# The fourth layer's Fourier mixer on scaled columns, with the token factor applied behind the feature stage, and a new order in the opening

## The reference

```python
def rms_norm(x, g, eps=RMS_EPS):
    x32 = x.astype(jnp.float32)
    y = x32 * lax.rsqrt(jnp.mean(x32 * x32, axis=-1, keepdims=True) + eps)
    return y.astype(x.dtype) * g

def modulate(x, g, shift, scale):
    return rms_norm(x, g) * (1 + scale) + shift

def fourier_mixer(h, w, bias):
    b, s, d = h.shape
    hg = h.astype(jnp.float32).reshape(b, s, FOURIER_GROUPS, d // FOURIER_GROUPS)
    f = jnp.fft.fft2(hg, axes=(1, 3), norm="ortho").real
    return f.reshape(b, s, d).astype(h.dtype) @ w + bias
...
        sh_a, sc_a, g_a, sh_m, sc_m, g_m = jnp.split(silu_c @ mod_w[i] + mod_b[i], 6, axis=-1)
        h_lat = modulate(x_lat, norm_mix_g[i], sh_a, sc_a)
...
        x_lat = x_lat + g_a * y_lat
        x_lat = x_lat + g_m * sq_relu_mlp(modulate(x_lat, norm_mlp_g[i], sh_m, sc_m), mlp_w1[i], mlp_w2[i])
```

## Time and profile before

| | us |
|---|---|
| executions | 2173.69, 2174.12, 2174.76 |
| median | 2174.12 |
| the profiled execution, its device time | 2173.29 |
| its span in the profile | 2171.4 |
| busy in the span: TensorE, VectorE, ScalarE, GpSimd | 2066.7, 1508.5, 1016.9, 9.2 |
| mean granted clock of TensorE | 0.972 |

### The profile page before, as it was taken

The page is one execution under the profiler, slowest core; times in us unless marked ns, Lnnn a source line. Parts: engine busy times, 40 slices in busy tenths (PEclk is TensorE's granted clock), DMA queues, the critical chain, the costliest instruction groups (busy, mean ns, idle before and its releaser), DMA issues.

```text
span 2171.4 us, 34465 instructions
## 1 busy us (share of the span) xinstructions
PE 2066.7 (95%) x13290; PEld 1832.1 (84%) x13290; DVE 1508.5 (69%) x2301; ACT 1016.9 (47%) x1691; POOL 9.2 (0%) x33
## 2 busy tenths in 40 slices
PE   6999999998999999999988889998999998999998
PEld 4698888887877788888866779998999987899998
DVE  3668668587667586857677868887866774555555
ACT  4362323237666562322336765555644653444443
POOL 0000000000000000000000000000000000000000
PEclk9999999999999999999998999999999997899999
DMA  8847445441112245558551128663465541355553
GB/s 312 304 172 226 145 157 166 153 131 60 59 59 78 86 152 189 176 178 274 186 152 62 35 62 307 233 234 123 156 195 175 164 148 39 117 175 174 174 175 106
DMA packets 254147, 340.37 MB, mean 157 GB/s; under 512 B 23895, under 2 KB 232626, under 8 KB 250946
## 3 DMA queue, kind: packets, MB, share of 16 engines
q1 hardware_dynamic: 254018, 338.60, 46.9%
HBM read 337.52 MB, written 1.05 MB: 156 GB/s over the span
## 4 chain that ended last, share of the span: by engine, by line
PE 79%; DVE 9%; ACT 7%; issue 4%; DMA 0%; SPq 0%; DVEq 0%; POOL 0%; ACTq 0%
PE bank L1624 24%; PE bank L1625 23%; PE bank L1626 23%; PE bank L2399 4%; DVE w_lo L2461 1%; ACT p_raw L1256 1%; PE bank L1676 1%; ACT w_hi L917 1%; DVE norm L2488 1%; ACT p_raw L1244 1%; DVE p_all L2945 1%; PE bank L1695 1%; ACT norm L1010 1%; ACT mp_raw L1422 1%; DVE neg_max L2954 0%
## 5 line engine op out<-in xcount | busy, mean ns | idle before, releaser
L917 ACT ACTIVATE w_hi<-w_raw 128x1024 fp32r<-128x1024 f32 x443 | 462.7, 1052 | 459.6 <-PE bank L1626 459.2
L2461 DVE TENSOR_TENSOR w_lo<-w_raw,w_hi 128x1024 fp32r<-128x1024 f32 x443 | 537.0, 1220 | 42.2 <-ACT w_hi L917 39.3
L1624 PE MATMUL bank<-g_hi,w_hi 128*128 128x256 f32 (+1 forms) x1728 | 549.5, 318 | 7.5 <-DVE g_lo L2999 3.6
L1625 PE MATMUL bank<-g_lo,w_hi 128*128 128x256 f32 (+1 forms) x1728 | 545.3, 316 | 0.0
L1626 PE MATMUL bank<-g_hi,w_lo 128*128 128x256 f32 (+1 forms) x1728 | 545.0, 315 | 0.0
L1624 PE MATMUL bank<-h_hi,w_hi 128*128 128x512 f32 (+3 forms) x1360 | 465.7, 342 | 13.7 <-DVE h_lo L2498 9.9
L1625 PE MATMUL bank<-h_lo,w_hi 128*128 128x512 f32 (+3 forms) x1360 | 459.1, 338 | 0.0
L1626 PE MATMUL bank<-h_hi,w_lo 128*128 128x512 f32 (+3 forms) x1360 | 458.9, 337 | 0.0
L1624 PEld LDWEIGHTS bank<-g_hi,w_hi 128*128 128x128 f32 x1728 | 330.8, 191 | 37.5 <-issue 6.0
L1626 PEld LDWEIGHTS bank<-g_hi,w_lo 128*128 128x128 f32 x1728 | 330.8, 191 | 20.5
L1625 PEld LDWEIGHTS bank<-g_lo,w_hi 128*128 128x128 f32 x1728 | 331.0, 192 | 19.4
(11 more groups left out here) (457 smaller groups left out, 2746.6 us busy)
## 6 DMA issues: line engine op xcount, KB each, us to landing
w_raw<-in_mlp_w SPq DMA_DIRECT2D x128, 1024.0 KB, 5.8
mod_raw<-in_mod_w SPq DMA_DIRECT2D x96, 768.0 KB, 4.7
first_raw<-in_mod_w SPq DMA_DIRECT2D x24, 1024.0 KB, 5.7
w_raw<-in_w_expert_gate SPq DMA_DIRECT2D x16, 1024.0 KB, 5.3
w_raw<-in_w_expert_up SPq DMA_DIRECT2D x16, 1024.0 KB, 5.6
w_raw<-in_w_expert_down SPq DMA_DIRECT2D x16, 1024.0 KB, 5.5
w_raw<-in_diff_w_qkv SPq DMA_DIRECT2D x12, 1024.0 KB, 5.1
w_raw<-in_fourier_w SPq DMA_DIRECT2D x8, 1024.0 KB, 5.7
```

Source lines behind the costliest of these rows:

```text
L917: act.activation(W_hi[n % RING][:, :].rearrange("p (k c) -> p k c", c=P), w_raw[slot][:, :, place, :], ACT.Copy).then_inc(s("w_hi"), 1)
L1624: pe.matmul(dst, w_hi, r_hi, start=start, stop=False)
L1625: pe.matmul(dst, w_hi, r_lo, start=False, stop=False)
L2461: dve.tensor_tensor(W_lo[n % RING][:, :].rearrange("p (k c) -> p k c", c=P), w_raw[slot][:, :, place, :], W_hi[n % RING][:, :].bitcast(F32 ...
```

## The change

In the fourth layer's mixer "mix3" joins the tuple LATE: each column of X is multiplied by its scale, without shift and without the token's factor, as soon as the third MLP has completed it. The feature tiles are made of these columns. token_sum sums the squares into two columns of one number per token, one root and one reciprocal of 128 x 2 follow (token_rstd), and the evacuation of the feature tiles (both parts) multiplies by it, since tokens lie in the partitions there. The shift is transformed by itself: waves_of_shift, six small products inside the last block of the third MLP, gives 8 columns of one number per feature, which are added to token 0 of each difference and sum.

In the opening the fold matrix is loaded ahead of the context; the norm of the rows is made for x first and for the context then; the row products start behind the second unit of the first group; the small vectors are turned behind the last unit of the group; the high and low part of the DFT matrix are made earlier; the scaled columns leave out the edge columns and are waited for one by one; GpSimd makes the low part of the eight output columns; of the three panels split ahead, two are split behind the last column; turning the second group follows the first output panel. SP issues the DFT matrix before the last three units of the first group, and the mixer's two weight units behind six units of the second group instead of ahead of it. ROW_NORMS goes from 6 to 8, the meta tokens' wait for meta_sum from 1 to 2, and the plan's tile counts follow.

```diff
--- before.py
+++ after.py
...
-LATE = ("mlp2", "mlp3", "win", "ffn_2")
+LATE = ("mlp2", "mix3", "mlp3", "win", "ffn_2")
...
-ROWS_AFTER = {2: range(0, 4), 3: range(4, 8), 4: range(8, 12), 5: range(12, 16)}
+ROWS_AFTER = {1: range(0, 3), 2: range(3, 6), 3: range(6, 9), 4: range(9, 12), 5: range(12, 14), 6: range(14, 16)}
 SCALED_AHEAD = [("scale", 0), ("scale", 1), ("sum", 0), ("scale", 2), ("sum", 1), ("scale", 3), ("sum", 2), ("sum", 3)]
-THIRD_GROUP_AT = {0: [0], 1: [1, 2], 2: [3, 4], 3: [5], 4: [6], 5: [7]}
+THIRD_GROUP_AT = {1: [0, 1], 2: [2, 3], 3: [4], 4: [5], 5: [6], 6: [7]}
...
+        shift_waves = sb("shift_waves", [P, 2, GROUPS])
+        token_rstd = sb("token_rstd", [P, 2])
...
+        U_hi = {"mlp2": H_hi, "mix3": H_hi, "mlp3": U3_hi, "win": H_hi[:, :, META:TOK2], "ffn_2": G_hi}
+        U_lo = {"mlp2": H_lo, "mix3": H_lo, "mlp3": U3_lo, "win": H_lo[:, :, META:TOK2], "ffn_2": G_lo}
...
+        def inner(v, m, st):
+
+            return v[:, m, st * LAT:(st + 1) * LAT].rearrange("p (e c) -> p e c", e=2)[:, :, 1:]
...
+            if name == "mix3":
+                return scale_mix[:, k, 0:1]
...
-            sp.dma_start(x_rows[:, 2:4, :], a["ctx"][0].rearrange("(t p) d -> p t d", p=P)).then_inc(s("x_in"), 16)
+            sp.dma_start(first_fold[:, :, :], a["first_fold"].rearrange("p (k c) -> p k c", k=2)).then_inc(s("ctx_in"), 16)
+            sp.dma_start(x_rows[:, 2:4, :], a["ctx"][0].rearrange("(t p) d -> p t d", p=P)).then_inc(s("ctx_in"), 16)
             load_first(range(FIRST_RING))
-            sp.dma_start(first_fold[:, :, :], a["first_fold"].rearrange("p (k c) -> p k c", k=2)).then_inc(s("fold_in"), 16)
...
-            load_first(range(FIRST_RING, MOD_UNITS))
+            load_first(range(FIRST_RING, MOD_UNITS - 3))
             dft_in = a["dft"].rearrange("(k p) (a c) -> p k a c", p=P, a=2)
             for k in range(2):
                 sp.dma_start(dft[:, 2 * k:2 * k + 2, :], dft_in[:, k]).then_inc(s("dft_in"), 16)
+            load_first(range(MOD_UNITS - 3, MOD_UNITS))
...
+            load_first(range(MOD_UNITS, 2 * MOD_UNITS - 2))
             for u in range(2):
                 load_unit(PLAN.at["four0"]["unit"] + u, [(whole, four_w[u])])
-            load_first(range(MOD_UNITS, 2 * MOD_UNITS))
+            load_first(range(2 * MOD_UNITS - 2, 2 * MOD_UNITS))
...
+            for n in range(KT):
+                pool.wait_ge(s("four_hi"), n + 1)
+                pool.tensor_tensor(H_lo[:, n, :], norm_buf[4 + n % 2][:, :], H_hi[:, n, :].bitcast(F32),
+                                   ALU.subtract).then_inc(s("four_lo"), 1)
...
+                    if n == 2 * KT - 3:
+                        act.wait_ge(s("dft_in"), 32)
+                        act.activation(dft_hi[:, :, :].rearrange("p k (a c) -> p (k a) c", a=2), dft[:, :, :],
+                                       ACT.Copy).then_inc(s("dft_hi"), 1)
+                tile = t + 2 * KT
+                act.wait_ge(s("tile_done"), tile + 1)
+                for v in range(1, VEC_TILES):
+                    ins = act.activation(vec[:, v, 0:VEC_COUNT[v]], bank[tile % BANKS][:, v * P:v * P + VEC_COUNT[v]], ACT.Copy)
+                ins.then_inc(s("vec"), 1)
                 copy_first_rows(0)
-                act.wait_ge(s("dft_in"), 32)
-                act.activation(dft_hi[:, :, :].rearrange("p k (a c) -> p (k a) c", a=2), dft[:, :, :],
-                               ACT.Copy).then_inc(s("dft_hi"), 1)
...
-                                c = slice(st * LAT, (st + 1) * LAT)
-                                act.activation(G_hi[:, m, c], four_raw[:, m, c], ACT.Identity,
+                                act.activation(inner(G_hi, m, st), inner(four_raw, m, st), ACT.Identity,
                                                scale=scale_mix[:, m, st:st + 1]).then_inc(s("u_hi"), 1)
...
                     if g == 3:
-                        copy_first_rows(1)
-                    if g == 2:
-                        for n in range(AHEAD):
-                            split_hi(PLAN.at["four0"]["panel"] + n)
+                        split_hi(PLAN.at["four0"]["panel"])
...
+                for n in range(1, AHEAD):
+                    split_hi(PLAN.at["four0"]["panel"] + n)
+                copy_first_rows(1)
...
-                                           ACT.Copy).then_inc(s("four_hi"), 1)
+                                           ACT.Identity, scale=token_rstd[:, i:i + 1]).then_inc(s("four_hi"), 1)
...
+                if layer == 2:
+                    act.wait_ge(s("scales_mix"), 4)
...
+            for st in range(2):
+                if st == 0:
+                    act.wait_ge(s("x_in"), 16)
+                else:
+                    act.wait_ge(s("ctx_in"), 32)
+                for i in range(2):
+                    tt = 2 * st + i
+                    if tt:
+                        act.wait_ge(s("row_norm"), 4 * st + i)
+                    act.activation(row_squares[:, :], x_rows[:, tt, :], ACT.Square,
+                                   accum_out=row_sum[:, tt:tt + 1]).then_inc(s("row_norm"), 1)
+                rows = slice(2 * st, 2 * st + 2)
+                act.wait_ge(s("row_norm"), 4 * st + 2)
+                act.activation(row_inv[:, rows], row_sum[:, rows], ACT.Sqrt, bias=eps[:, 0:1],
+                               scale=1.0 / D).then_inc(s("row_norm"), 1)
+                if st == 0:
+                    act.wait_ge(s("ctx_in"), 32)
+                    act.activation(first_fold_hi, first_fold[:, :, :], ACT.Copy).then_inc(s("dft_hi"), 1)
+                act.wait_ge(s("row_norm"), 4 * st + 4)
+                for tt in (2 * st, 2 * st + 1):
+                    act.activation(rows_hi[:, tt, :], x_rows[:, tt, :], ACT.Identity,
+                                   scale=row_inv[:, tt:tt + 1]).then_inc(s("u_hi"), 1)
...
-            mod_norm("mix3", 3, LAT)
...
+            act.wait_ge(s("sum"), SUM_AT["mix3"] + 1)
+            act.activation(token_rstd[:, :], sum_ps[:, 2 * GROUPS:2 * GROUPS + 2], ACT.Sqrt, bias=eps[:, 0:1],
+                           scale=1.0 / D).then_inc(s("root"), 1)
+            act.wait_ge(s("rstd"), SUM_AT["mix3"] + 1)
...
+                    if (stage, g) == (1, 0):
+                        token_sum()
...
-                turn_first(1)
...
-                    for u in THIRD_GROUP_AT[m]:
+                    if m == 0:
+                        turn_first(1)
+                    for u in THIRD_GROUP_AT.get(m, []):
...
+            def waves_of_shift():
+
+
+                pe.wait_ge(s("scales_mix"), 4)
+                for part in range(2):
+                    dst = sum_ps[:, part * GROUPS:(part + 1) * GROUPS]
+                    for k in range(2):
+                        ins = pe.matmul(dst, dft_late[:, 2 * k, 0:P], mod[3][:, k:KT:2, 0], start=(k == 0), stop=(k == 1))
+                for k in range(2):
+                    ins = pe.matmul(dst[0:1, :], dft_late[:, 2 * k, P:P + 1], mod[3][:, k:KT:2, 0], start=(k == 0), stop=(k == 1))
+                ins.then_inc(s("meta_sum"), 1)
...
+            def token_sum():
+
+                pe.wait_ge(s("sq_added"), SQ_AT["mix3"] + KT)
+                for i in range(2):
+                    ins = pe.matmul(sum_ps[:, 2 * GROUPS + i:2 * GROUPS + i + 1], norm_buf[2][:, i * P:(i + 1) * P], ones[:, 0:1],
+                                    start=True, stop=True)
+                ins.then_inc(s("sum"), 1)
...
+                            if last and layer == 2 and j == KT:
+                                waves_of_shift()
...
-                if u == 1:
+                if u == MOD_UNITS - 1:
...
-            norm_sum("mix3", LAT)
...
-                dve.wait_ge(s("dft_hi"), 2)
-                dve.tensor_tensor(dft_lo[:, :, :].rearrange("p k (a c) -> p (k a) c", a=2), dft[:, :, :],
-                                  dft_hi[:, :, :].bitcast(F32).rearrange("p k (a c) -> p (k a) c", a=2),
-                                  ALU.subtract).then_inc(s("dft_lo"), 1)
...
-                                c = slice(st * LAT, (st + 1) * LAT)
-                                ins = dve.scalar_tensor_tensor(G_lo[:, m, c], four_raw[:, m, c], scale_mix[:, m, st:st + 1],
-                                                               G_hi[:, m, c].bitcast(F32), ALU.mult, ALU.subtract)
-                        ins.then_inc(s("edge"), 1)
-                        dve.wait_ge(s("edge"), g + 4)
+                                dve.wait_ge(s("u_hi"), 5 * g + 4 + 2 * (m - 2 * g) + st + 1)
+                                dve.scalar_tensor_tensor(inner(G_lo, m, st), inner(four_raw, m, st), scale_mix[:, m, st:st + 1],
+                                                         inner(G_hi, m, st).bitcast(F32), ALU.mult, ALU.subtract)
+                        dve.wait_ge(s("u_hi"), 5 * g + 9)
...
-                    if g == 2:
-                        for n in range(AHEAD):
-                            split_lo_at(p0 + n)
+                    if g == 3:
```

(41 more changed lines are left out.)

74 lines of the change are left out of this document (26 added, 48 removed).

## The result

The changed kernel took 2155.34 us (median of four executions, 2155.27 to 2157.11) against 2174.44 for the kernel before (2173.69 to 2176.58): ratio 0.9912, 95% interval 0.99 to 0.9925. In a second set the changed kernel took 2156.75 against 2172.74, ratio 0.993, 0.9916 to 0.9943: 16.0 us less. The two profiled executions differ by 18.0 us of span (2171.4, 2153.4).

The account below looks back on a forecast made before the run. TensorE, carrying 79% of the chain, was taken to bound the kernel, with gains only where it stands still. Mixer 9.1 plus opening 3.0 made 12.1 us, from 2174.1 to 2162.0 for the median, range 2156 to 2168.

Parts of the forecast that it names:

- The mixer, removed and new order: Fourth layer's mixer: normalisation waits vanish, column stage starts at 1500.8 instead of 1510.05, output panels 9.1 us earlier.
- The opening, the rows: Opening's row products start 3.3 us earlier, the first group's last unit ends 1.7 us earlier, DFT starts at 45.65.
- The DFT stage and the hole: Opening: two weight units in the DMA queue delay the seventh unit 4 us; stage still ends 3.0 us earlier.
- The rule weighed: Opening: GpSimd's subtraction may contend with VectorE for SBUF, up to 10 us of VectorE's time; costed at nothing.
- The sum: Whole kernel: mixer 9.1 plus opening 3.0 gives 12.1 us less, 2162.0 for the median.
- What follows is TensorE without holes, so all of it stays: Behind the fourth layer's mixer: the whole 9.1 us gain reaches the end.
- Behind it the same products and eight units follow: Behind the opening's DFT stage: work continues as before and units land before they are asked for, keeping 3.0 us.
- The baseline: Whole kernel before: the profiled execution took 2173.3 us, 0.8 under the median of 2174.1.
- The rivals: Other outcomes, in the opening, the mixer's clock or loads, or GpSimd: 2155.9 to 2177.4 us, chances 0.03 to 0.18.
- No hole for the units: Opening's DFT stage: weight units don't delay the seventh unit, opening gains 9.1 us, total 2155.9; chance 0.18.

Follow-up runs that it names:

- the mixer's part alone: All of the diff that belongs to "mix3", put on the kernel before with its opening unchanged: 2163.89 us against 2172.69, ratio 0.9953.
- the parts run alone: Mixer's and opening's shares of the diff, each separately on the kernel before: 2163.89 us (ratio 0.9953) and 2167.98 us (ratio 0.9978).
- a delay: 12 transposes more at turning the second group's sums: changed kernel 2159.7 us; kernel before, same addition, 2174.8 against 2173.89.
- a larger delay: Changed kernel with the four transposes of the second group's sums made nine times more (thirty-six more): 2162.33 us.
- the kernels without the hole: Changed kernel with mixer's weight units ahead of the second group: 2152.24 us; also low part on VectorE, 2151.79, or with fillers, 2150.71, 2150.48, 2150.18.

## Why the prediction was wrong, point by point

- *The mixer, removed and new order.* Right: the column stage starts 4.5 us after TensorE is free (forecast 4.7), 11.4 us from there to the panels as forecast, no cost of the late scaling (162.28 us from 1329.26 to 1491.54, against 161.15, the waves' 1.13 more). The shift's waves were put at 1.4 and took 1.1. 9.7 us instead of 9.1, within the bounds of 7.5 to 10.4.
- *The opening, the rows.* Right within half a microsecond: row products 20.30 (forecast 19.85), last unit 39.19 (39.7), DFT 45.46 (45.65).
- *The DFT stage and the hole.* Right: 4.25 us (forecast 4), half clock for one pair, end at 74.46 (74.9). 3.39 us instead of 3.0. Loading the two megabytes ahead of the group showed the cause. That the size fits so well is in part luck: with the same opening and the mixer of before, the hole was 5.31 us and the gain 1.35, and the opening of before came out 1.2 us later in another execution. GpSimd's subtraction took 1.28 (1.29).
- *The rule weighed.* The contention is there (up to 1.0 us a time), its cost is not (0.05 us behind the first mixer), as the sum had it.
- *The sum.* This is the step that failed. "What follows is TensorE without holes, so all of it stays" and "Behind it the same products and eight units follow" take it that code behind the change runs as it did; the first is also wrong as it stands, since the trace of the kernel before has eight waits of 0.7 to 3.8 us behind the mixer. The code there has the same instructions, but the clock around its waits came out otherwise: 4.9 us of the 18.0 between the traces. The sum put that at nothing without a reason, and the range had no width for it. How much such steps can make is shown by the mixer's part alone: 4.2 us in the third layer's attention, ahead of its edit.
- *The baseline.* The profiled execution of before lay 0.8 us under its median of then, 1.2 under that of the full set; that of the changed kernel on its median. Later sets gave before 2172.7 to 2173.9.
- *The rivals.* "No hole for the units" names 2155.9, almost the time measured, and is false: the hole is there. A right total is no evidence of a mechanism.

So the two places explain 13.1 us (13.5 by the parts run alone), and the rest of the 16 to 19 is half clock at unchanged places that is longer or shorter. What is shown is that the granted clock differs at the steps looked at, that the changed kernel has the shorter stretches in both of its traces, and that fillers take half clock away in the two waits of 3.2 and 7.55 us. That a delay brings the steps back is seen in one trace, and a larger delay didn't. Why the changed kernel comes out better, and at which times a wait is followed by half clock, stays open; so does why the executions of before spread by 7 us and those of the kernels without the hole by 0.6 to 5.

## What to carry to other kernels

Compare two traces by marks, the same wait in both, and not by totals: a difference that changes between two marks of identical code is not the change's. Where a kernel has waits of 1.5 us and more behind the change, give the range some microseconds for the clock behind them, and don't believe a gain of that size, from a filler above all, until traces of several kernels without the change lack it at the same mark. Look up what lies between two loads of a ring in the queue before moving anything there: two megabytes held TensorE back by 6.7 us here, of which 3.3 were left at the end.

## What the runs showed that I had not expected

Less work can gain nothing (1.4 us earlier, 0.07 later one mark on). The same code takes one of a few times: 583.1 to 583.4 us or 584.0 to 584.2 from the first mixer to the second layer's mark in thirteen of the fourteen traces, 72.2 to 72.5 or 73.7 to 74.0 behind the meta tokens' sum. So a gain of 0.8 or 1.6 us there is no sign of an edit. Products that nobody reads, in a wait, keep the clock at 1.00, and that can save time or not: 22 transposes ahead of the DFT stage saved 1.0 to 2.4 us, 20 transposes and six large products around the wait of 7.55 us nothing that these traces show. Transposes of 128x128 follow each other every 0.113 us. Beside GpSimd's subtraction four columns of VectorE take 2.69 us instead of 1.68, and GpSimd's pair 2.78 instead of twice 1.28.
